# Tile 0's rows of the last two expert slots combined on TensorE, and the first block of the next layer moved inside both ways of a branch

## What is computed

```python
def hier_moe(x, g2, r_g, r_e, w_gate, w_up, w_down):
    h = rmsnorm(x, g2).reshape(b * t, d)
    ...
    gates = jnp.sum(jax.nn.one_hot(eidx, N_EXP) * (gw[:, None] * tw)[..., None], axis=1)   # two of 16 are not zero
    a = jax.nn.silu(jnp.einsum('nd,edf->nef', h, w_gate)) * jnp.einsum('nd,edf->nef', h, w_up) * gates[..., None]
    return jnp.einsum('nef,efd->nd', a, w_down).reshape(b, t, d)
...
xp = xp + hier_moe(xp, ...)                 # then, in the next layer:
z = rmsnorm(x, g1) @ w_in
```

## Time and profile before

| | us |
|---|---|
| median of three runs | 936.6 (935.08 to 937.87) |
| the profiled execution: its own time | 937.48 |
| its span, first to last instruction | 935.7 |
| TensorE busy | 894.7 |
| VectorE, ScalarE, GpSimd busy | 400.9, 242.6, 185.8 |
| mean granted TensorE clock, as a share of full speed | 0.987 |

### The profile page before, as it was taken

How to read it: one execution, slowest core, us unless ns; L and a number is a source line. 1 busy time by engine, 2 the same in 40 slices (tenths; PEclk the granted TensorE clock), 3 DMA queues, 4 the chain that set the end, 5 groups by cost and what they waited for, 6 DMA issues and landing times.

```text
span 935.7 us, 13401 instructions
## 1 busy us (share of the span) xinstructions
PE 894.7 (96%) x4836; PEld 432.5 (46%) x4836; DVE 400.9 (43%) x1039; ACT 242.6 (26%) x495; POOL 185.8 (20%) x259
## 2 busy tenths in 40 slices
PE   9999999999999999989799999999999999999991
PEld 6444355556546544333444344455564464433330
DVE  2403225577538646111163032357764575741123
ACT  3211256643102021111131113566420111211110
POOL 2243201331101111110035042013312011111100
PEclk9999999999999999999999999999999999999996
DMA  9716004351015999999583060043410179999996
GB/s 344 288 56 258 23 1 134 97 173 55 2 45 210 339 413 410 420 418 379 219 321 116 4 278 1 0 142 103 169 46 23 63 297 360 421 386 420 420 350 240
DMA packets 38619, 197.48 MB, mean 211 GB/s; under 512 B 6520, under 2 KB 6648, under 8 KB 22672
## 3 DMA queue, kind: packets, MB, share of 16 engines
q1 hardware_dynamic: 19456, 136.04, 36.2%
q0 software_dynamic: 14736, 45.72, 14.2%
q10 hardware_dynamic: 4352, 14.76, 4.4%
HBM read 175.16 MB, written 27.79 MB: 217 GB/s over the span
## 4 chain that ended last, share of the span: by engine, by line
PE 86%; DMA 7%; DVE 4%; issue 2%; ACT 2%; ACTq 0%; DVEq 0%; SPq 0%; POOLq 0%; POOL 0%
PE ps L729 78%; PE ps L727 7%; DMA vc<-in_w 4%; DMA cat<-y_rows 1%; DMA hT<-h_rows,igat 1%; PE ps L745 1%; DMA y_rows<-hn,isca 1%; DVE hT L1608 0%; DVE tmp L1686 0%; DVE tmp L1741 0%; DVE hT L2182 0%; ACT L1430 0%; ACT L1384 0%; ACT L1418 0%; ACT ring L1418 0%
## 5 line engine op out<-in xcount | busy, mean ns | idle before, releaser
L729 PE MATMUL ps<-ring,hT 128*128 128x512 f32 (+4 forms) x1200 | 404.2, 583 | 5.9 <-DMA vc<-in_w 2.7
L729 PEld LDWEIGHTS ps<-ring,hT 128*128 128x128 f32 (+2 forms) x1200 | 153.6, 158 | 210.0 <-issue 206.4
L729 PE MATMUL ps<-ring,cat 128*128 128x512 f32 (+3 forms) x496 | 211.0, 598 | 0.0
L729 PEld LDWEIGHTS ps<-ring,cat 128*128 128x128 f32 (+2 forms) x496 | 74.2, 168 | 80.8 <-issue 79.1
L2182 DVE TENSOR_TENSOR hT<-ps,par 128x512 f32<-128x512 f32 x48 | 31.1, 686 | 131.0 <-PE ps L727 126.0
L670 POOL DMA_INDIRECT y_rows<-hn,isca x24 | 24.1, 1004 | 214.9 <-ACT hn L1512 210.5
L549 POOL TENSOR_TENSOR st<-st,half 128x1 f32<-128x1 f32 (+3 forms) x60 | 63.0, 1050 | 11.1 <-POOL st L547 10.7
L1629 DVE TENSOR_REDUCE st<-sqj 128x8 f32<-128x512 f32 x20 | 13.5, 681 | 111.5 <-ACT sqj L1346 111.4
L547 POOL TENSOR_SCALAR st<-st 128x1 f32<-128x1 f32 (+3 forms) x60 | 16.3, 272 | 222.6 <-DVE st L1629 81.7
L729 PE MATMUL ps<-hT,ring 128*128 128x512 f32 x128 | 57.1, 599 | 0.7 <-DVE tmp L1686 0.7
L1512 ACT COPY hn<-ps 128x1024 f32<-128x1024 f32 x22 | 22.3, 1012 | 87.6 <-PE ps L729 81.6
(11 more groups left out here) (295 smaller groups left out, 1080.2 us busy)
## 6 DMA issues: line engine op xcount, KB each, us to landing
ring<-in_w SPq DMA_DIRECT2D x80, 1024.0 KB, 11.3
kc<-in_w SPq DMA_DIRECT2D x12, 1024.0 KB, 15.6
vc<-in_w SPq DMA_DIRECT2D x12, 1024.0 KB, 15.8
v<-in_w SPq DMA_DIRECT2D x10, 1024.0 KB, 14.3
kva<-in_w SPq DMA_DIRECT2D x10, 1024.0 KB, 14.7
kc<-in_ck POOLq DMA_DIRECT2D x32, 256.0 KB, 3.7
vc<-in_cv POOLq DMA_DIRECT2D x32, 256.0 KB, 3.2
h_rows<-qk ACTq DMA_DIRECT2D x10, 512.0 KB, 2.6
```

Source lines behind the costliest of these rows:

```text
L729: ins = pe.matmul(out, lhsT, rhs, start=start, stop=stop, skip_group_check=loose)
```

## The change

For tile 0 the high rows are put together from two sources. The rows of slots up to 9 are loaded from `y_rows` (`ahead_in`) by ScalarE in iteration 11, behind the landing of slot 9's scatter, and added with the gate `gE` (zero where the token's higher expert lies in slots 10 or 11, or in an extra slot). GpSimd holds slot 10's scatter until that load has landed. The rows of slots 10 and 11 are taken straight from `y_sb`: VectorE builds a matrix of ones and zeros for each of the two slots (`late_hot`, slot row to token row), TensorE multiplies it with `y_sb` in two column halves into banks S0 and S1, and VectorE adds the banks with the token's gate. Small sums on VectorE (`inl`, `gE`, `gX`, `rowl`) give the gates. Tile 0's high load behind the last scatter is gone from the way without extra slots, in both layers. The part of `y_rows` that tile 0 reads is blanked too at the start.

`unless` takes the place of `only_if` in `extras`: the way without extra slots is written first, the way with them second, and a `finish` is built into both: on TensorE tile 0's block of the next layer (`next_tile`), on VectorE the two increments that release it (`first_ready`). The filler `keep_busy(14, "I")` is gone.

```diff
+def unless(eng, name, none, some, body, finish, arrivals=(), uncounted=(), otherwise=None):
...
+    with eng.If(none):
+        if not arrivals:
+            eng.drain()
+        if otherwise:
+            otherwise()
+        for c in before:
+            end = before[c] + totals[key][c.name]
+            if end != c.local and c not in uncounted:
+                if c in arrivals:
+                    eng.wait_ge(c.sem, c.now())
+                eng.sem_inc(c.sem, end - c.local)
+                c.local = end
+        finish()
+    ends = {c: c.local for c in Count.every}
+    with eng.Else():
+        for c in before:
+            c.local = before[c]
+        body()
+        finish()
...
-    only_if(eng, n_extra > 0, first, otherwise=otherwise, **moved)
+    unless(eng, name, n_extra < 1, n_extra > 0, first, finish, otherwise=otherwise, **moved)
...
+        BY_PRODUCTS = (NSLOT - 2, NSLOT - 1)
...
-                    for t in range(NT):
-                        pool.dma_start(y_rows[TOK + t * P:TOK + (t + 1) * P, :], blank).then_inc(*blank_out.inc(by=16))
+                    for at in (0, *(TOK + t * P for t in range(NT))):
+                        pool.dma_start(y_rows[at:at + P, :], blank).then_inc(*blank_out.inc(by=16))
...
+                    if n == BY_PRODUCTS[0]:
+                        wait(*ahead_in.at("ahead"))
                     scatter(n % 2, isca[:, n:n + 1], ("m", n), y_out[n % 2])
...
-                if l:
-                    keep_busy(14, "I")
...
-                rows("k", 0)
+                rows("k", 0, l, range(1 if l else 0, TP))
...
+                for hf in range(2):
+                    claim(f"S{hf}")
+                    for i, n in enumerate(BY_PRODUCTS):
+                        pe.wait_ge(*dve_s.at("by", i))
+                        pe.wait_ge(*read[("J", "I")[hf] if i else "O"].at("down", "m", n))
+                        mm(bank(f"S{hf}"), late_hot[i], y_sb[:, n % 2, hf * W:(hf + 1) * W], start=(i == 0), stop=(i == 1),
+                           inc=full[f"S{hf}"].inc("by", hf) if i else None)
                 flush()
                 n_extra = extra_slots(pe, "pe")
+
+                def next_tile():
+                    if l + 1 < L:
+                        Count.layer = l + 1
+                        rows("k", 0, l + 1, (0,))
+                        Count.layer = l
...
                 for n in range(NSLOT + 1):
                     if 1 <= n < NSLOT:
                         act_turned((n - 1) % 2, ("m", n - 1))
+                    if n == BY_PRODUCTS[1]:
+                        for b in range(2):
+                            act.wait_ge(*y_out[b].at("y", "m", last_slot(b, BY_PRODUCTS[0])))
+                        act.dma_start(y_high[:, 0, :], y_rows[0:P, :]).then_inc(*ahead_in.inc("ahead", by=16))
                     if n < NSLOT:
                         silu(n % 2, ("m", n))
...
                     scattered_mains()
-                    for t in range(NT):
+                    for t in range(1, NT):
...
+                    for i, s in enumerate(BY_PRODUCTS):
+                        if s in GROUPS[g]:
+                            link(vec.tensor_scalar(stat["rowl"][:, i:i + 1], work[:, s - s0:s - s0 + 1], SKIP + 1.0, None, ALU.add))
+                            vec.tensor_tensor(late_hot[i], stat["rowl"][:, i:i + 1].to_broadcast([P, P]), iota[:, 0:P], ALU.is_equal).then_inc(*dve_s.inc("by", i))
...
+                    here, past, gate = stat["gE"], stat["gX"], stat["gAB"][:, 0:1]
...
+                add_rows(0, stat["gE"], y_high, ahead_in.at("ahead")).then_inc(*dve_s.inc("ahead"))
+                dve.wait_ge(*dve_s.at("ahead"))
+                for hf in range(2):
+                    dve.wait_ge(*full[f"S{hf}"].at("by", hf))
+                    cols = x[:, 0, hf * W:(hf + 1) * W]
+                    vec.scalar_tensor_tensor(cols, bank(f"S{hf}"), stat["gAB"][:, 0:1], cols, ALU.mult, ALU.add).then_inc(*read[f"S{hf}"].inc("by", hf))
+
+                def first_ready():
+                    dve.sem_inc(*x_half.inc())
+                    dve.sem_inc(*x_ready.inc())
...
-                    if t == 0 and l + 1 < L:
-                        dve.wait_ge(*high_in[0].at("high"))
-                        for hf in range(2):
-                            cols = slice(hf * W, (hf + 1) * W)
-                            ins = vec.scalar_tensor_tensor(x[:, 0, cols], y_high[:, 0, cols], stat["gAB"][:, 0:1], x[:, 0, cols], ALU.mult, ALU.add)
```

More of the change, by code:

```diff
@@ L173, in only_if, with extras @@
     eng.nop()
-def extras(eng, n_extra, slot, done=None, otherwise=None, start=None, **moved):
+def unless(eng, name, none, some, body, finish, arrivals=(), uncounted=(), otherwise=None):
+    before = {c: c.local for c in Count.every}
+    totals = Count.every[0].totals
+    key = ("branch", name, Count.layer)
+    if key not in totals:
+        only_if(eng, some, body, arrivals=arrivals, uncounted=uncounted, otherwise=otherwise)
+        totals[key] = {c.name: c.local - before[c] for c in before}
+        finish()
+        return
+    with eng.If(none):
[16 more added lines that the diff above has]
+        body()
+        finish()
+    for c in before:
+        c.local = ends[c]
+    eng.nop()
+def extras(eng, name, n_extra, slot, done=None, otherwise=None, start=None, finish=lambda: None, **moved):
     def pair(key, number, q):
@@ L519, in load @@
                                      ).then_inc(*landed[SLOT[i]].inc("w", i, by=16))
-                extras(sp, n_extra, load, arrivals=landed)
+                extras(sp, "sp", n_extra, load, arrivals=landed)
             for t in range(NT):
@@ L775, in turn_input @@
                     elif t == 0:
[L776 to L779 removed]
+                        pe.wait_ge(x_half.sem, l)
+                        turn_rows("h1", 0, (x_ready.sem, l * NT + 1))
                         return
@@ L793, in weight, with rows @@
                     return ring[:, bass.DynSlice(spill_in[i[1]], 1), at:at + W].rearrange("p a n -> p (a n)")
-                def rows(name, c):
-                    for t in range(TP):
+                def rows(name, c, l, tiles=range(TP)):
+                    for t in tiles:
                         u = f"S{t % 2}"
@@ L1303, in extra_index @@
                         index_rows(g)
-                extras(pe, n_extra, slot, start=extra_index)
+                extras(pe, "pe", n_extra, slot, start=extra_index, finish=next_tile)
         @block.scalar
@@ L1573, in load_high @@
                         high_load(t)
-                extras(act, n_extra, slot, done=load_again, otherwise=load_high)
+                extras(act, "act", n_extra, slot, done=load_again, otherwise=load_high)
         @block.vector
@@ L2113, in late_gates @@
                     link(vec.tensor_tensor(lower, lower, late, ALU.subtract))
+                    here, past, gate = stat["gE"], stat["gX"], stat["gAB"][:, 0:1]
+                    link(vec.scalar_tensor_tensor(work[:, 0:E], win[:, 0:E], 0.5, selA[:, 0:E], ALU.is_gt, ALU.mult))
+                    link(vec.tensor_reduce(past, work[:, 0:E], AX.X, ALU.add))
+                    link(vec.tensor_reduce(here, stat["inl"], AX.X, ALU.add))
+                    link(vec.tensor_tensor(here, here, past, ALU.add))
+                    link(vec.tensor_tensor(here, here, gate, ALU.mult))
+                    link(vec.tensor_tensor(here, gate, here, ALU.subtract))
+                    link(vec.tensor_tensor(past, past, gate, ALU.mult))
                 def spill_place(over, cap):
@@ L2239, in add_late @@
                 def add_late():
+                    for hf in range(2):
+                        dve.wait_ge(*read[f"S{hf}"].at("by", hf))
+                    link(add_rows(0, stat["gX"], y_high, high_in[0].at("high")))
                     for t in range(NT):
@@ L2247, in extra_index @@
                         index(g)
-                extras(dve, n_extra, slot, done=add_late, start=extra_index)
+                extras(dve, "dve", n_extra, slot, done=add_late, start=extra_index, finish=first_ready)
                 def add_high(t):
```

37 lines of the change are left out of this document (18 added, 19 removed).

## The result

The changed kernel takes 948.7 us (median of four runs, 945.45 to 949.75); the kernel before takes 937.2 beside it. The ratio is 1.0114, with a 95% interval from 1.0081 to 1.0147. It is slower by some 11 us, above the range of the prediction. The profiled execution took 949.61, its span is 947.9: 12.2 more than before.

What follows compares the result with a forecast made beforehand. It took TensorE, busy 86% of the span, as the bound, with only its waits to gain; -3.2 + 0.4 + 0.1 + 4.7 + 1.4 - 1.9 + 0.2 + 0.1 = +1.8 on 936.6 gave 938.4 us, range 932.0 to 942.0.

Steps and rivals of the forecast that it cites:

- The seam: Between the layers: tile 1's matmuls start earlier, -3.2 us; tile 2's turn waits for tile 3's high load, +0.4.
- Tile 0's start: At the seam: tile 0's transposes start at about 462 instead of 466.75, its matmuls at 463.5 instead of 468.24.
- VectorE's turn of tile 1: At the seam: tile 2's high add ends at 472.0, first half of the turn done at 472.7; TensorE waits 1.2 us.
- rival B: Seam: TensorE's jump over the other way's code, now behind tile 0's matmuls, adds 3.0 us, giving 941.4; chance 0.18.
- The stall in layer 1: Layer 1's end: slot 11's silu waits for slot 9's scatter, moving its transposes from 908.91 to 913.6, +4.7 us.
- The low clock behind it: Layer 1, after TensorE's idle stretch: the first 2.2 to 3.4 us of work run at half speed, +1.4 us.
- The tail: Kernel end: four loads instead of five behind the last landing, -1.9 us; ScalarE's loads wait for TensorE's count, +0.2.
- GpSimd's wait for the ahead load: Ahead of slot 10's scatter, both layers: POOL's new wait for the load costs nothing, 0 us.
- VectorE's small edits and layer 0's silu: Index, one-hot and gate helpers on VectorE, +0.1 us; layer 0's silu moves to about 449.25, mostly hidden, +0.1.
- chance for slower: Whole kernel above 939.4 us: 0.35, from the forecast 0.14, the jump rival 0.15 and the late-tile-0 rival 0.06.

Runs made afterwards that it cites:

- e6: The changed kernel with the ahead load issued by SyncE instead of ScalarE and no branch on TensorE: 936.8 us, 0.9995 of the kernel before.
- e8: The kernel before the change with TensorE's branch taken away: 939.3 us, 1.0023 of the kernel before.
- e3: The changed kernel with TensorE's branch taken away: 941.6 us, 1.0048 of the kernel before.
- e5: e2 with the old filler of 14 identity products put behind tile 0's block, ahead of the jump: 944.3 us, 1.0073 of the kernel before.
- e7: e6 with the change kept in layer 0 only: 933.8 us, 0.9963 of the kernel before.
- e2: The changed kernel with the ahead load issued by SyncE instead of ScalarE: 939.7 us, 1.0026 of the kernel before.
- e4: The changed kernel with the change kept in layer 0 only: 942.2 us, 1.0051 of the kernel before.
- e11: The changed kernel with four of layer 1's five low loads moved behind the silu of slot 11: 940.1 us, 1.0028 of the kernel before.
- e1: The changed kernel with tile 0's block (TensorE) and the releasing increments (VectorE) put behind the branch: 944.5 us, 1.0070 of the kernel before.
- e9: The changed kernel with the change in layer 0 only and the ahead load on SyncE, inner block kept: 940.7 us, 1.0041 of the kernel before.

## Why the prediction was wrong

It forecast +1.8 and the span grew by 12.2. By its own terms, from the profiled executions:

**The seam, -3.2 + 0.4, measured +2.6.** Tile 0's start (462 and 463.5; 461.37 and 462.82) and VectorE's turn of tile 1 (472; 472.73) were right, and e6 shows the gain that follows from them, 3.1. The step that failed is the one that left the jump out of the sum and made it rival B. That rival was right as a mechanism. Its size, 4.2, comes near the gap (4.47, 4.29 and 4.10 in three kernels) by luck: the 2.75 and 1.41 us that it was read from the earlier trace rows hold 1.31 us that stay without a branch (e8), and the gap is what is left of the jump behind the 2.8 us of tile 1's transposes and tile 0's last four matmuls. What was wrong was to expect two thirds of it to hide and to leave the rest out of the sum: VectorE's turn of tile 1 was ready with the first half at about 473.4, and TensorE went on at 477.22, 3.8 us later. In the gap, 472.9 to 477.1, the queues of the kernel after show one packet of code:

```profile
q0 software_dynamic: 111, 0.64, 62.8%
q10 hardware_dynamic: 112, 0.37, 38.3%
q8 instruction: 1, 0.02, 1.9%
```

The Trainium skill (Runtime: NRT & Kernel Launch, Instruction fetch mechanics) says that a taken branch whose target lies outside the window already fetched has to wait for a DMA fetch of it. The trace agrees: no branch, no gap (e3, e6). All six kernels that keep the inner block show a packet on queue q8 2.9 to 3.0 us ahead of tile 1's matmuls (in the kernel after at 474.2, in e5, behind the filler, at 476.9), and e3, e6 and e7 show none between tile 0's matmuls and tile 1's. Here the jump leads over a part of the code that never runs. Behind it came a second term that the sum did not have: the clock fell in the pause, and tile 1's matmuls lost 1.5 us (6.89 for 12 instructions; 7.05 in e2, 5.39 in e6 at the same place). A third is small: the ahead load took 8.2 us to land in layer 0 (issued at 449.09, behind the first of SyncE's 1 MB weight loads) and held slot 10's scatter to 458.39, slot 11's by 2.2 us and ScalarE's first load by 1.0. I had given it till 454.4 from a landing of some 5 us that no row had shown. In e2, issued ahead of those weight loads, it took 3.4.

**The stall in layer 1, +4.7, measured 4.4 idle, 5.1 by the distance to slot 9's scatter.** Right, by its reason too: e2 and e4 take it away, e11 shows that the low loads make the scatter slow.

**The low clock behind it, +1.4, measured +2.8.** The mechanism was right and the size was off. I took the length of the slow stretch, 2.2 to 3.4 us, from the one recovery in the trace of before, which shows the 3.4; no row gives the 2.2. In the kernel after the high clock was back 5.7 us behind the first instruction, in e1 and e3 3.2 and 4.5. It differs from one kernel's execution to the next, and the largest is 1.7 times my upper bound.

**The tail, -1.9 + 0.2, measured 0.0.** The sum took the third load's landing over and cut off what stood behind it. But the four loads then landed later: at +4.2, +8.1 and +10.6 instead of the third at +7.35, and tile 0's store, set free at 931.2 when its adds end, is issued at 931.89, beside the loads, and not ahead of them. That this is what holds the loads is likely and not shown: the tail is shortest (17.63) in e6, where the store is issued 2.3 us ahead of them, but 18.68 in e1, where it comes 0.9 behind. Over all kernels the tail with four loads takes 18.7 us on average (seven of them, 17.6 to 19.6), with five 19.6 (seven, 18.4 to 20.2): a gain of 0.9, about half of the forecast, against a loss of 8.0 in the whole end.

**GpSimd's wait for the ahead load, 0.** Wrong in both layers. In layer 0 it held slot 10's scatter in the changed kernel itself, as said above. In layer 1 it shows once the stall is gone: e2 and e6 have slot 10's scatter held, and 2.0 and 2.6 us more between slots 9 and 11, against tails that are, with a load fewer, 1.2 and 2.0 shorter. The step looked only at the times with the stall in them.

**VectorE's small edits and layer 0's silu, +0.2.** Up to 456.0 the two spans agree within 0.1: nothing. The miss of 10.4 us is so made up: seam 5.4, end of layer 1 3.6 (4.4 forecast, 8.0 measured), and 1.5 in the middle of layer 1, which lies within the spread of the kernels there.

The prediction's chance for slower, 0.35, was the result, but its range ended at 942. The range took each rival alone; the stall was in the forecast and B was a rival to it, so that both at once (938.4 + 3.0), with the clock behind the second pause (1.7 by e2) and twice as much behind the first (1.4), would have come to 944.5, outside it.

## What to carry to other kernels

When code is moved to the other side of a branch, price the jump where it will stand. Here it was covered where the engine had to wait for data anyway; with work that counts behind it, 4 us of it lay open, and 28 short filler products ahead of it covered next to nothing. Before moving a load forward, ask which engine waits for it in program order, and what stands behind that wait; the load belongs on an engine with nothing behind it, and even there each wait that protects the buffer has to be followed to the next scatter. In these runs a pause of TensorE of 4 us and more cost its length and then again 1.5 to 3 us at the low clock.

## What the hardware showed that I had not expected

- The clock fell at about 463.2 in the changed kernel although TensorE had only short pauses in the stretch before (1.54 and 0.39 us between its rows); it did so in e5 too (7.08 for 12 instructions), and in e2 and e6, with the same pauses, the 12 at that place ran in 5.39, at full speed. Behind the long pauses it came back 3.0 to 5.7 us after work began again (477.22 to 480.25 and 918.25 to 924.0 in the kernel after).
- A taken branch on TensorE cost 4.3 to 4.5 us of idle time behind matmuls at full speed (e2 and after), 2.5 to 2.7 where the work just ahead of it ran slow (e9, e11, e4), and 4.1 with 28 more instructions ahead of it (e5).
- Taking a jump out of the kernel before made it 0.2% slower (1.0006 to 1.0041). The pause that it opened brought the low clock; most of the loss lies elsewhere and is not explained.
- A scatter of 128 rows of 4 KB took 6.1 us to land with 0.38 MB of loads on queue q10 (ScalarE's) beside it (e11), and 9.2 with 1.63 MB of them (the kernel after).
